# Local attention and the output stage put into one block, with the undilated steps' second half last and the first operands of the output stage loaded beside them

## The reference, cut to what matters

```python
q = rmsnorm(q.reshape(b, s, 8, 64), q_norm_w)          # 8 heads of 64
k = rmsnorm(k.reshape(b, s, 8, 64), k_norm_w)
for window, dilation in ((128, 1), (512, 4), (2048, 16)):
    # each query attends to i + dilation*j, |j| <= 64, swept in blocks of 128 queries
    # logits = q.k/8 + rel_bias[bucket]; p = exp(logits - max); o = p@v / sum(p)
    o_i, lse_i = dilated_window_attention(q, k, v, rel_bias, window, dilation)
mix = jax.nn.softmax(jnp.stack(lses, axis=0), axis=0)    # over the 3 dilations
o = jnp.einsum('gbsh,gbshd->bshd', mix, jnp.stack(outs, axis=0))
y_attn = o.reshape(b, s, 512) * jax.nn.silu(z_attn)
y = jnp.concatenate([y_conv, y_attn], axis=-1)
x = x + jnp.einsum('bse,ed->bsd', y, w_out)
```

## Time and profile before

| | us |
|---|---|
| median of 3 runs | 3156.92 |
| lowest and highest | 3152.03, 3160.36 |
| the profiled execution | 3157.81 |
| its span in the trace | 3155.7 |
| mean granted TensorE clock, share of full | 0.962 |

### The profile page before, as it was taken

The page is one execution under the profiler, slowest core; times in us unless marked ns, Lnnn a source line. Parts: engine busy times, 40 slices in busy tenths (PEclk is TensorE's granted clock), DMA queues, the critical chain, the costliest instruction groups (busy, mean ns, idle before and its releaser), DMA issues. The chain is left out here.

```text
span 3155.7 us, 78648 instructions
## 1 busy us (share of the span) xinstructions
PE 2894.3 (92%) x35058; PEld 2393.1 (76%) x35058; DVE 1602.7 (51%) x2633; ACT 1081.3 (34%) x2002; POOL 606.9 (19%) x412
## 2 busy tenths in 40 slices
PE   7999999999778888888887999999999997999699
PEld 4887888887377778777875778888777895777487
DVE  6432232433177777777754662222577105767662
ACT  3223332322644545545443441000222104546310
POOL 5522222110013223233221120000000001134230
PEclk9999999999979999999888999999999998999899
DMA  5123321211833233233216772011122216223672
GB/s 171 61 78 119 107 98 56 87 51 46 273 92 105 70 97 110 71 97 98 69 30 196 234 175 69 20 41 34 47 71 69 80 42 215 77 74 108 222 247 84
DMA packets 342032, 322.79 MB, mean 102 GB/s; under 512 B 14095, under 2 KB 257167, under 8 KB 341056
## 3 DMA queue, kind: packets, MB, share of 16 engines
q1 hardware_dynamic: 313104, 258.31, 27.0%
q10 hardware_dynamic: 24480, 47.21, 4.2%
q0 software_dynamic: 4112, 12.25, 1.5%
HBM read 199.77 MB, written 122.64 MB: 102 GB/s over the span
## 5 line engine op out<-in xcount | busy, mean ns | idle before, releaser
L331 PE MATMUL pj_ps<-pj_x_hi,pj_w_hi 128*128 128x512 f32 x1024 | 402.7, 393 | 10.6 <-DVE pj_w_lo L280 5.6
L331 PE MATMUL pj_ps<-pj_x_hi,pj_w_lo 128*128 128x512 f32 x1024 | 399.9, 390 | 0.0
L331 PE MATMUL pj_ps<-pj_x_lo,pj_w_hi 128*128 128x512 f32 x1024 | 399.7, 390 | 0.0
L1830 PE MATMUL dm_ps<-h_hi,dm_w_hi 128*128 128x512 f32 x896 | 279.5, 393 | 0.0
L1830 PE MATMUL dm_ps<-h_hi,dm_w_lo 128*128 128x512 f32 x896 | 275.9, 389 | 0.0
L1830 PE MATMUL dm_ps<-h_lo,dm_w_hi 128*128 128x512 f32 x896 | 275.8, 389 | 0.0
L221 POOL TENSOR_TENSOR pj_x<-h 128x512 f32<-128x512 f32 x128 | 166.8, 1304 | 486.6 <-DVE pj_x_lo L275 437.3
L275 DVE TENSOR_TENSOR pj_x_lo<-pj_x,pj_x_hi 128x512 fp32r<-128x512 f32 x128 | 91.7, 716 | 320.3 <-ACT pj_x_hi L350 320.2
L331 PEld LDWEIGHTS pj_ps<-pj_x_hi,pj_w_hi 128*128 128x128 f32 x1024 | 193.3, 189 | 54.7 <-DVE pj_w_lo L280 8.2
L331 PEld LDWEIGHTS pj_ps<-pj_x_lo,pj_w_hi 128*128 128x128 f32 x1024 | 193.4, 189 | 41.0 <-issue 1.0
L331 PEld LDWEIGHTS pj_ps<-pj_x_hi,pj_w_lo 128*128 128x128 f32 x1024 | 192.9, 188 | 40.5
(11 more groups left out here) (256 smaller groups left out, 5918.7 us busy)
## 6 DMA issues: line engine op xcount, KB each, us to landing
proj<-pj_out ACTq DMA_DIRECT2D x128, 256.0 KB, 2.5
pj_w<-w_in SPq DMA_DIRECT2D x32, 512.0 KB, 4.1
proj<-lr_out SPq DMA_DIRECT2D x32, 512.0 KB, 5.0
dm_w<-w_out SPq DMA_DIRECT2D x32, 512.0 KB, 5.0
dm_w<-w_in SPq DMA_DIRECT2D x32, 512.0 KB, 4.8
partial<-wa_ob SPq DMA_DIRECT2D x48, 264.0 KB, 2.1
mo_part<-partial SPq DMA_DIRECT2D x16, 792.0 KB, 9.1
wa_vt<-v_rows SPq DMA_DIRECT2D x43, 260.0 KB, 3.0
```

The costliest lines, as they stand in the source:

```text
L331: mm = pe.matmul(ps[i][:], wp, xp, start=k == 0 and m == 0, stop=k == KT - 1 and m == len(parts) - 1)
L1830: last = pe.matmul(PS[:, 2 * i + b, :], wp, hp[:, k, t0:t0 + 512], start=k == 0 and m == 0, stop=k == KT - 1 and m == len(parts) - 1)
```

## The change

The two stages become one block, `attention_and_output`. `window_attention` is split into `window_buffers`, which allocates, and `window_programs`, which returns one function for each engine; the output stage calls these first and then goes on in its own program, with no barrier between. Four things go with this.

1. `window_steps` puts undilated steps 0 to 7 first, then the 32 dilated ones, then undilated steps 8 to 15. One tile of values at the cut is loaded twice (54 loads for 53).
2. The buffers are laid out anew: `mo_part` lies over the tables of the dilated steps and `wa_qs`, `wa_ks`; `mo_w_hi0`, `mo_w_lo0`, `mo_y_hi0`, `mo_y_lo0`, `mo_conv`, `mo_w0` and `mo_w1` lie over nothing of the attention. The rest lies over buffers that the last steps still use, and gets waits (`window_read`, `scores_read`, `values_read`, `outputs_stored`, `dilated_read`).
3. A function `beside(t)` is called within the steps on SP, DVE and ACT. With NS = 48: SP loads weight tile 0, convolution block 0 and weight tile 1 at t = 40, parts 0 and 1 at t = 42, weight tile 2 at t = 44. ACT casts weight tile 0 at t = 41 and the four pieces of the convolution at t = 42 to 45, and takes the exponents of parts 0 and 1 at t = 44 and 46. DVE does the `small` work of parts 0 and 1 in halves at t = 44 to 47. The low parts of weight tile 0 and of convolution block 0 are made by POOL and not by DVE.
4. PE does the turns of b = 0 behind (0, j, FIRST) for j = 1, 2, 4, 5 (before: 3, 4, 5, 5). DVE and ACT get another order for weight tiles 1 to 5.

```diff
@@ window_steps @@
-    def residue(g, first, length):
+    def residue(g, first, length, part):
...
+        start, stop = (part * blocks // 2, (part + 1) * blocks // 2) if part is not None else (0, blocks)
-        for n in range(blocks + 1):
+        for n in range(start, stop + 1):
...
+    residue(0, 0, T, 0)
     for g, dil in enumerate(DILATIONS):
-        for r in range(dil):
-            residue(g, r, T // dil)
+        if g:
+            for r in range(dil):
+                residue(g, r, T // dil, None)
+    residue(0, 0, T, 1)
@@ sync @@
-            load_w(0)
-            load_conv(0)
-            load_w(1)
-            load_part(0)
-            load_w(2)
-            load_part(1)
+            def beside(t):
+                if t == NS - 8:
+                    load_w(0)
+                    load_conv(0)
+                    load_w(1)
+                if t == NS - 6:
+                    dilated_read(sp)
+                    outputs_stored(sp, NS - 8)
+                    load_part(0)
+                    load_part(1)
+                if t == NS - 4:
+                    load_w(2)
+
+            window_sync(sp, beside)
+            window_read(sp)
             load_z(0)
             for j in range(3, KT):
                 load_w(j)
                 if j == 3:
                     load_conv(1)
+            outputs_stored(sp, NS)
             for n in range(RING):
                 load_res(n)
             load_part(2)
@@ gpsimd @@
+            window_gpsimd(pool)
+            pool.wait_ge(s_w_hi, 1)
+            pool.tensor_tensor(w_lo[0][:], w[0][:], w_hi[0][:], ALU.subtract).then_inc(s_w_lo, 1)
+            for k in range(CB):
+                pool.wait_ge(s_conv_hi, k + 1)
+                pool.tensor_tensor(y_lo[0][:, k, :], conv[:, k, :], y_hi[0][:, k, :], ALU.subtract).then_inc(s_conv_lo, 1)
@@ vector: beside, and what follows the steps @@
+            def beside(t):
+                if t == NS - 4:
+                    lowest(0)
+                if t == NS - 3:
+                    shares(0)
+                if t == NS - 2:
+                    lowest(1)
+                if t == NS - 1:
+                    shares(1)
+
+            window_vector(dve, beside)
+            values_read(dve)
+            weighted(0, 0)
+            dve.wait_ge(s_w_lo, 1)
             weights(1)
+            weighted(0, 1)
             weights(2)
-            small(0)
...
+            outputs_stored(dve, NS)
             for i in range(4):
                 gate(0, i)
                 if i < 2:
                     weighted(0, i + 2)
+                if i < 3:
+                    weights(i + 3)
                 low(0, i)
             weights(6)
             weights(7)
             small(2)
@@ tensor @@
+            window_tensor(pe)
+            scores_read(pe)
             pe.wait_ge(s_conv_lo, CB)
             for j in range(BANKS):
                 pe.wait_ge(s_w_lo, j + 1)
                 products(0, j, FIRST)
-                if j >= 3:
-                    turn(0, j - 3)
-            turn(0, 3)
+                if j == 1:
+                    window_read(pe)
+                if j in (1, 2):
+                    turn(0, j - 1)
+                if j in (4, 5):
+                    turn(0, j - 2)
             pe.wait_ge(s_lo, 4)
@@ scalar @@
+            def beside(t):
+                if t == NS - 7:
+                    weights(0)
+                if NS - 6 <= t < NS - 2:
+                    conv_high(0, t - NS + 6)
+                if t == NS - 4:
+                    exponent(0)
+                if t == NS - 2:
+                    exponent(1)
+
+            window_scalar(act, beside)
+            for j in (1, 2, 3):
+                weights(j)
+            high(0, 0)
+            weights(4)
+            high(0, 1)
+            weights(5)
+            for i in (2, 3):
+                high(0, i)
             weights(6)
             weights(7)
```

More of the change, by code:

```diff
@@ L2095, in window_attention @@
     NV, NO = 8, 6
[L2096 to L2136, removed]
@@ new lines, in window_programs, with sem @@
+    table, qk, vt, sc, p, pt, ob, qs, ks, S_PS, P_PS, O_PS = buffers
+    def sem(n):
+        return sems.new(f"wa_{n}")
+    s_qk = [sem(f"qk{b}") for b in range(4)]
+    s_table = [sem(f"table{g}") for g in range(NG)]
+    s_vt = [sem(f"vt{i}") for i in range(NV)]
+    s_out = [sem(f"out{i}") for i in range(NO)]
+    s_stage, s_scores, s_reduced, s_exps, s_turned, s_weights, s_values, s_copied = (
+        sem(n) for n in ("stage", "scores", "reduced", "exps", "turned", "weights", "values", "copied"))
@@ L2138, in store, with gpsimd @@
+    def gpsimd(pool):
+        pool.wait_ge(s_skew, 16 * NG)
+        for g in range(NG):
+            heads = slice(g * HEADS, (g + 1) * HEADS)
+            pool.dma_start(table[g][:], skewed[:, heads, 0:256]).then_inc(s_table[g], 16)
+        for b in range(4):
+            pool.wait_ge(s_qk[b], 32)
+        for n, t in enumerate(STAGED):
             g, w, col, q0, k0, parts = STEPS[t]
             dil = DILATIONS[g]
[L2140 to L2142 removed]
@@ L2144, in _ @@
[L2144 to L2159, removed]
-                    source = v_rows[first:first + dil * (rows - 1) + 1:dil, :]
-                    sp.dma_start(vt[loaded % NV][0:rows, :], source).then_inc(s_vt[loaded % NV], 16)
-                    loaded += 1
-                if t >= 1:
-                    store(sp, t - 1)
-            store(sp, NS - 1)
-            for i in range(NO):
-                sp.wait_ge(s_out[i], 16 * (NS // NO))
@@ new lines, in scalar, with exps, copy @@
+    def scalar(act, beside):
+        def exps(t, n):
+            g, w, col, q0, k0, parts = STEPS[t]
+            u, jj = 2 * t + n // 2, n % 2
+            pair = 4 * t + n
+            act.wait_ge(s_reduced, pair + 1)
+            if pair >= 4:
+                act.wait_ge(s_turned, pair - 3)
+            for m in range(2):
+                h = 2 * n + m
+                last = act.activation(p[u % 2][:, jj, m, 0:w], sc[u % 2][:, jj, m, 0:w], ACT.Exp,
+                                      bias=ob[t % NO][:, h, DH + 1:DH + 2], scale=-1.0)
+            last.then_inc(s_exps, 1)
+        def copy(t, hf):
+            act.wait_ge(s_values, 4 * t + 2 * hf + 2)
+            act.copy(ob[t % NO][:, 4 * hf:4 * hf + 4, 0:DH + 1],
+                     O_PS[hf][:, 0:4 * (DH + 1)].rearrange("p (h e) -> p h e", e=DH + 1)).then_inc(s_copied, 1)
+        for t in range(NS):
+            exps(t, 0)
+            exps(t, 1)
+            if t > 0:
+                copy(t - 1, 1)
+            exps(t, 2)
+            exps(t, 3)
+            copy(t, 0)
+            beside(t)
+        copy(NS - 1, 1)
```

546 lines of the change are left out of this document (285 added, 261 removed).

## The result

| | before | after |
|---|---|---|
| median, us | 3160.30 | 3143.46 |
| lowest and highest of 20 runs | 3152.03, 3174.24 | 3137.79, 3160.40 |
| the profiled execution | 3157.81 | 3155.12 |

A forecast was written before the change was run, and what follows sets the result against it. PE was taken as the bound in the attention and after REST, with waits and half clock between. 0 + 0.5 - 22.7 + 1 = -21.2 us took the profiled 3157.8 to 3136.6, given as 3136; range 3127 to 3147.

The forecast's parts named there:

- order of the steps: Attention's 48 steps: the new order costs nothing, only the drain at the end differs; 0, with 1 us to either side.
- work beside the last steps: Work inserted on ACT and DVE in the attention's last steps, mostly hidden behind PE: 0.5 us, with ends of 0 and 4.
- attention's end to REST: From the attention's last matmul to REST of b = 0: 28.1 us for 50.8, so -22.7, between -25.7 and -14.7.
- REST to REST of b = 1: After REST begins, part 2's load stands behind weight tile 7, delaying DVE's `small` some 3 us: +1, from 0 to +4.
- the signs that the prediction set for itself: First product under 0.5 us behind; steps 6.9 to 7.2 us; REST within 26 to 31, next 35 to 38, then 132.
- rival A: Before REST, weight tile 3 and all behind it still wait for buffers and DMA: 6 to 8 us more, 3143; chance 0.2.
- an insertion below that is hidden in the main: Attention's steps: insertions shorter than the mean wait for PE per step, DVE 1.6 us and ACT 2.7, are mostly hidden.
- Rival C: Last steps: ACT waits for a weight or convolution transfer, PE behind it; slower, 3162 if it lands after 35 us; chance 0.04.
- The clean chain: From the attention's end, DVE operations at mean lengths without contention: w4 at 14.8 us, REST at 25.1, the lower bound.
- added 3 us for it, late tiles and clock together: Before REST: 3 us on top of 25.1 for DVE beside POOL's adds, late weight tiles 3 to 5 and the clock.
- B: Before REST, contention and clock cost nothing, and nothing comes back afterwards: -25.7 us, so 3131; chance 0.15.
- D: After the attention, PE's first products still wait a whole round; REST at 40 us or later, 3149; chance 0.06.

The follow-up runs named there:

- the warm-up: Changed kernel with 100 transposes of the identity on PE ahead of the first scores: 3142.20 us, 19.5 us from first scores to store of step 1.
- new order alone: The kernel before with the new order of steps and nothing else: 3168.99 us, last eight steps 53.7 us.
- nothing beside the steps: Changed kernel with the output stage's loads and its ACT and DVE work moved behind the last step: 3172.26 us, 48.1 us from attention's end to REST.
- the exponents had moved: Changed kernel with the exponents of parts 0 and 1 at t = 45 and 47, not 44 and 46: 3145.67 us, last eight steps 54.6 us.
- the loads alone: Changed kernel with only SP's loads beside the steps, casts, low parts and small operations behind the last step: 3153.63 us, 42.2 us to REST.
- part 2 early: Changed kernel with part 2 loaded ahead of weight tiles 6 and 7 in SP's queue: 3150.05 us, REST to REST of b = 1 35.2 us.
- five edits: Changed kernel with later exponents, paired convolution casts, part 2 loaded earlier, 100 transposes and DVE's new order: 3144.51 us, against 3154.58 on the same chip.
- POOL's adds small: Changed kernel with POOL's eight adds of b = 0 on one head of eight: 3137.42 us, 28.6 us from attention's end to REST.
- DVE's queue reordered: Changed kernel with low parts of tiles 3, 4 and 5 ahead of the `weighted` or `gate` before them: 3151.72 us, 28.9 us to REST.

## Why the forecast came out as it did

| term, us | forecast | profile pair | of it shown by an experiment |
|---|---|---|---|
| ahead of the attention | 0 | +1.6 | none |
| clock at its start | 0 | +7.9 | it comes and goes, with the warm-up too |
| order of the steps | 0 | 0 | new order alone: 0 |
| work beside the last steps | +0.5 (0 to 4) | +4.5 | 2.5 is `exponent` a step too early; 1.5 is half clock, open |
| attention's end to REST | -22.7 (-25.7 to -14.7) | -19.7 | 2.1 by DVE's order, or 2.5 by POOL's adds |
| REST to REST of b = 1 | +1 (0 to +4) | +3.1 | 3.4 by part 2's load |

The second and fourth rows are parted by the store of step 1. Against the 53.7 us of the kernels with nothing beside the steps, the fourth is +4.9 and the second +7.5.

The sign, the places and the main mechanism were right: loads and splits hide under a full PE, the first product follows at once, DVE's chain sets REST, and part 2 gives something back. Three terms were too small, each by 2 to 4 us and all to one side. They make -12.1 in the profile pair (the first two rows left out), where -21.2 was forecast. The 20 runs say 12.3 to 20.5, between the two, with either just outside. The second measurement of the changed kernel, on another chip, gives 12.3 us by its ratio (8.2 to 16.5), which fits the -12.1 and not the -21.2.

Of the signs that the prediction set for itself, the first product without a gap and the last 132 us came. The other three were just missed: the last eight steps 7.3 us each (6.9 to 7.2), REST at 31.1 (26 to 31), the next REST another 38.6 (35 to 38). And the median of 3143.5 lies in the band that was given to rival A (3140 to 3147), not in the forecast's own (3133 to 3140), although A's cause is not what the traces show. That it lies in the whole range owes something to luck: the range was made wide for late tiles, and other losses filled it.

**The attention's steps.** The step that failed is "an insertion below that is hidden in the main". It set the durations against the idle time of ACT and DVE, an average over 48 steps, and did not ask where in the step the inserted instruction stands and whom it waits for. `exponent(0)` is 0.24 us of work and cost 1.69 us of idle PE, `exponent(1)` another 0.88. Rival C had this form, ACT standing in midstep with all exponents behind it, but for a transfer: it looked at the DMA and not at DVE. That contention would hit two operations by 1.1 us was nearly right (0.90 and 0.97 in place of about 0.2).

**From the attention's end to REST.** The clean chain had w4 at 14.8 us; it ended at 18.6 (2965.1 against 2946.5). The prediction named the contention at 1.1 us a time and then added 3 us for it, late tiles and clock together. In the trace six of DVE's nine long operations to w4 took 0.5 to 1.1 us more, 5.3 in sum. Of these 1.5 did not reach w4: `weighted` began at 0.1 and not at 0.6, the chain had 0.2 us of gaps, and in the trace neighbouring DVE operations overlap by some 0.08 us each. And after a wait of 2.59 us seven matmuls went at 0.63 to 0.79 us in place of 0.4 to 0.5. So the term was mis-sized: it was 6.0 us in after (31.1 less 25.1), and 7.6 in the traces with more half clock ahead of REST. Rival A falls: tile 3, issued at 2949.58, was cast at 2954.47, 4.9 us later and not 12.4, and DVE was busy without a gap until 2966.8. Only with the contention gone do the loads show, with 1.29 us. B, the clean chain, falls as well, and D: REST came at 31, far from 40.

**After REST begins.** The cause was named (part 2 in SP's queue behind tile 7), its effect put at +1, as if DVE's slack took the rest. DVE's wait was 3.10 us, and nearly all of it went on the end.

## What to carry to other kernels

Work put beside a full engine cost little here by its duration (0.9 us, 54.6 against 53.7, once the exponents had moved) and more by its place in an in-order queue (2.5 us): for each inserted instruction ask whose result it needs, when that is ready within the step, and what stands behind it. A long serial stretch behind a busy one is best moved whole, since here the loads alone brought 5.9 us and the work on three engines 11.1. When a chain on DVE beside GpSimd is summed, take the contended durations for every operation with both inputs in SBUF from the start, not a lump for all.

## What the runs showed of the hardware

- DVE beside POOL adds or subtractions, both inputs in SBUF: 0.19 became 0.90, 1.22 became 2.29, 1.75 became 2.25 to 2.84. POOL lost as much: one add took 1.27 to 1.30 alone, and six of the eight here 2.2 to 2.7.
- In three of thirteen traces (after, part 2 early, five edits) PE stayed near half clock for the first 20 us or more of the attention, though busy 17.70 of 18.00 us; the store of step 1 came 27 to 28 us after the first scores and not 20 to 21. In two of the three PE had been idle for about 20 us ahead of it, but so it had in others that ran up within the first steps. In the third it had made 100 transposes and been idle for 2.92 us (in the trace with 100 transposes that ran at full, for 1.31 us). What decides it is open; it is worth 7 to 8 us and part of the spread of the times.
- In step 44 an idle of 1.69 us was followed by half clock in two traces (after, twice) and by the full clock in four (POOL's adds small, part 2 early, 100 transposes, DVE's queue reordered). The length of the idle alone does not decide it. A stretch of half clock of this kind cost about 1.5 us.
